# Reordering the projections around a long-convolution chain, with turns of four, later gates, a shorter root and interleaved last tiles, in a two-layer hybrid mixer and MoE kernel

## The reference

```python
h = modulate(layer_norm(x))                      # adaLN shift and scale, per stream
z = h @ w_in                                     # A: q 512, k 128, v 128; B: q, k, v 256 each; C: 3 x 256
A = dense_attention(rope(rms(q)), rope(rms(k)), v)      # 8 heads, 2 kv heads
B = neighbourhood_attention(q, k, v, rpb)               # 4 heads
x0, x1, v = split(short_conv(z_C, 3 taps))              # C: hyena
u = v * x1;  C = (long_conv(u, filters) + u * skip) * x0     # by transforms of length 512
x = layer_norm(alpha * x + gate * (concat(A, B, C) @ w_out))
```

## Time and profile before

| | us |
|---|---|
| median of 3 runs | 1529.31 (1528.60 to 1532.37) |
| the profiled execution, its own time | 1529.05 |
| its span, first to last instruction | 1527.2 |
| mean granted TensorE clock | 0.928 |
| PE busy | 1320.1 (86%) |
| VectorE, ACT, GpSimd busy | 538.8, 290.7, 303.7 |

### The profile page before, as it was taken

One profiled execution on the slowest core, in us unless ns is written; L12 is line 12 of the kernel. 1 busy time (PEld: TensorE's weight loads), 2 busy tenths in 40 slices (PEclk: granted clock), 3 DMA queues, 4 the chain that ended last, 5 costly groups with the idle time before them and its releaser, 6 DMA issues. The chain is left out here.

```text
span 1527.2 us, 19670 instructions
## 1 busy us (share of the span) xinstructions
PE 1320.1 (86%) x6420; PEld 733.0 (48%) x6421; DVE 538.8 (35%) x1346; ACT 290.7 (19%) x711; POOL 303.7 (20%) x395
## 2 busy tenths in 40 slices
PE   4999997788879999989889689994985799999991
PEld 1443433444445566656556434473543554545440
DVE  5205014456574322213222109245457221111124
ACT  0100001433210122212222211112520011111110
POOL 0000001445203133323232200100610411111000
PEclk9899997899897999999999989997996799999995
DMA  9767669000225899999998296423023799999930
GB/s 339 289 265 283 240 249 309 1 1 1 97 97 187 322 375 376 366 374 373 384 377 331 105 349 257 172 99 101 1 97 124 263 399 387 402 407 400 408 143 28
DMA packets 109724, 373.32 MB, mean 244 GB/s; under 512 B 17946, under 2 KB 24348, under 8 KB 100408
## 3 DMA queue, kind: packets, MB, share of 16 engines
q1 hardware_dynamic: 85752, 313.51, 54.5%
q0 software_dynamic: 23008, 55.40, 9.8%
q10 hardware_dynamic: 864, 3.15, 0.5%
HBM read 368.78 MB, written 30.47 MB: 261 GB/s over the span
## 5 line engine op out<-in xcount | busy, mean ns | idle before, releaser
L1239 PE MATMUL bank<-weights,b_qk 128*64 128x256 f32 (+2 forms) x1040 | 160.2, 384 | 4.4 <-DVE b_qk L2114 2.5
L1239 PEld LDWEIGHTS bank<-weights,b_qk 128*64 128x64 f32 (+2 forms) x1040 | 110.9, 147 | 63.9 <-issue 36.5
L2120 DVE TENSOR_TENSOR expert_act<-silu_a,bank 128x128 f32<-128x128 f32 x76 | 21.9, 288 | 310.7 <-ACT silu_a L1529 310.7
L1271 PE MATMUL bank<-tokens_h,a_k 128*128 128x512 f32 x208 | 103.7, 622 | 0.0
L1261 PE MATMUL bank<-weights,expert_act_T 128*64 128x512 f32 (+2 forms) x260 | 91.8, 617 | 8.6 <-DMA weights<-in_exp_w 4.9
L2308 POOL DMA_INDIRECT shift_scale_gate_norm<-scratch_h,gather_index x82 | 84.8, 1034 | 71.3 <-POOL gather_index L2305 66.6
L1239 PE MATMUL bank<-features_h,b_qk 128*32 128x256 f32 (+2 forms) x512 | 95.2, 381 | 0.4
L1059 PE MATMUL bank<-weights,features_h 128*128 128x512 f32 x192 | 86.2, 604 | 0.8 <-ACT features_h L1342 0.8
L2114 DVE COPY b_qk<-bank 128x512 f32<-128x512 f32 x78 | 53.9, 692 | 80.7 <-PE bank L1227 80.6
L1227 PE MATMUL bank<-tab,shift_scale_gate_norm 128*128 128x128 f32 x624 | 82.2, 275 | 0.0
L1529 ACT ACTIVATE silu_a<-bank 128x128 f32<-128x128 f32 x76 | 21.1, 278 | 315.0 <-PE bank L1239 315.0
(11 more groups left out here) (325 smaller groups left out, 2021.4 us busy)
## 6 DMA issues: line engine op xcount, KB each, us to landing
weights<-in_exp_w SPq DMA_DIRECT2D x195, 512.0 KB, 10.4
shift_scale_gate_norm<-in_ada_w SPq DMA_DIRECT2D x48, 1024.0 KB, 6.7
features_h<-in_exp_w SPq DMA_DIRECT2D x64, 512.0 KB, 9.7
qkv<-in_exp_w SPq DMA_DIRECT2D x64, 512.0 KB, 15.0
a_q<-in_exp_w SPq DMA_DIRECT2D x32, 512.0 KB, 12.4
weights<-in_w_in SPq DMA_DIRECT2D x6, 2048.0 KB
shift_scale_gate_norm<-scratch_mod POOLq DMA_DIRECT2D x16, 512.0 KB, 8.9
probs_T<-in_exp_w SPq DMA_DIRECT2D x16, 512.0 KB, 15.5
```

Of the source, the lines that this page charges most:

```text
L1239: mm = pe.matmul(ab[r, 0:2 * HIDDEN].rearrange("p (m h) -> p m h", m=2), XGT[:, u.slot() % 2, k, r], expert_w13(slot)[:, :, k, :], start=k ...
L1271: mm = pe.matmul(ACC[g][h][:, :], GROW[:, u.slot() % 2, g * P:(g + 1) * P], YSB[:, u.slot() % 2, h * HALF:(h + 1) * HALF], start=False, st ...
L2120: tt(ACTV[:, :], SIL[:, :], ab[:, HIDDEN:2 * HIDDEN], ALU.mult).then_inc(L["act"], 1)
```

## The change

1. **Order around the hyena chain.** Ring order of w_in becomes 0, 1, 3, 4, 2. The c products stand before the b products; the b products 0 and 1 behind the q/k transposes, 2 behind the transposes of u, 3 behind the first scores, and `yh` behind that, on all engines. The short convolution works f by f as each c product is drained. x0 and u lie in the free half of piece 4's ring slot, x1 in the `probs` tile. The slot is given back to w_out only when `yh` has been drained. The 40 adaLN steps of n = 1 to 5 are spread 2, 3, 2 to 3, 3 per product; `ADAB` lies in the router's tile, so router_w is loaded after the last group is filled.
2. **Turns of four.** `more` is rounded to whole turns, one test stands around four bodies, and layer 0's first overflow block (`ALWAYS = (1, 0)`) stands in `SEQUENCE[0]`. With these inputs no turn is run in either layer.
3. **Gates behind choices (layer 1).** The one-hots come first, 8 x 62 columns; GpSimd makes only the products with the choices; VectorE multiplies with the gates; PE does the 16 choice products, then the shared expert's second product, then the 16 gate products. GpSimd's zeroing of the gather tiles stands before its waits.
4. **Shorter root.** 8 steps instead of 11 for single tiles.
5. **Last tiles.** A signal per tile from PE, tiles 2 and 3 interleaved on VectorE, each written in two halves.

The diff, cut to its core:

```diff
+ALWAYS = (1, 0)
+BLOCKS = tuple(n + EXTRA + UNROLL for n in UNITS)
+    for n in range(ALWAYS[l]):
+        seq.append((UNITS[l] + n, [(x + n, EXPERTS + n)]))
+ADA_Q, ADA_KV, ADA_C, ADA_BQK = (2, 2, 2, 2), (3, 3, 3, 3), (2, 2, 2, 2, 3, 3), (3, 3, 0, 0)
...
-        items += [("win", l, b) for b in range(5)] + [("mixc", l), ("wo", l, 0), ("wo", l, 1)]
+        items += [("win", l, b) for b in (0, 1, 3, 4, 2)] + [("mixc", l), ("wo", l, 0), ("wo", l, 1)]
...
+                if n >= RING and items[n - RING][0] == "win" and items[n - RING][2] == 4:
+                    sp.wait_ge(by_vector, jobs.of[("yh", items[n - RING][1], 1)][2])
+                            sp.wait_ge(ada_filled, DEPTH * ADA_GROUPS)
...
-                if l == 0:
-                    for k in range(KD):
-                        ada(5, k)
-                    pe.wait_ge(ada_read, DEPTH * ADA_GROUPS)
...
+                queries_keys(0)
+                queries_keys(1)
                 pe.wait_ge(u_ready, l + 1)
+                u_rows = gate_and_u(l)
...
+                queries_keys(2)
                 read_out(("uT", l, full[-1]))
...
                 for i in range(n + PV_LAG):
                     if i < n:
                         scores(i)
+                    if i == 0:
+                        queries_keys(3)
+                        long_conv()
+                        read_out(("bqk", l, 3))
+                    if l == 0 and i == PV_LAG:
+                        pe.wait_ge(ada_read, DEPTH * ADA_GROUPS)
...
-                dve.wait_ge(by_scalar, jobs.of[("c", l, 5)][2])
+                for f, z in enumerate((*x0, *x1, *us)):
+                    dve.wait_ge(by_scalar, jobs.of[("c", l, f)][2])
...
                 with pe.Fori(0, EXTRA_TURNS) as i:
-                    for c in range(every, every + UNROLL):
-                        with pe.If(i * UNROLL + (c - every) < more):
+                    with pe.If(i * UNROLL < more):
+                        for c in range(every, every + UNROLL):
...
+                free(ts(turns, b[0:1, LISTED - EXPERTS:LISTED - EXPERTS + 1], float(UNROLL - 1 - ALWAYS[l]), float(EXTRA), ALU.add,
+                        ALU.min))
+                link(ts(turns, turns, int(math.log2(UNROLL)), None, ALU.logical_shift_right))
+                link(ts(turns, turns, int(math.log2(UNROLL)), None, ALU.logical_shift_left))
...
-                if l == DEPTH - 1:
-                    for _ in gates_of_choices():
-                        pass
+                if l == DEPTH - 1:
+                    gates = gates_of_choices()
+                    for _ in range(TOP_K):
+                        next(gates)
+                    gated(0)
+                    shared_act(nt - 1, full[-1])
...
+                if summed:
+                    for _ in gates:
+                        pass
+                    gated(1)
...
+            def rsqrt_steps(var, t):
+                xh, y, w = NV[:, t:t + 1], RS[:, t:t + 1].bitcast(F32), NT[:, t:t + 1]
+                yield ts(xh, var, -0.5, -0.5 * EPS, ALU.mult, ALU.add)
+                yield ts(RS[:, t:t + 1], xh.bitcast(I32), -0.5, float(0x1EF759DF), ALU.mult, ALU.add)
+                for _ in range(3):
+                    yield stt(w, y, xh, y, ALU.mult, ALU.mult)
+                    yield stt(y, w, 1.5, y, ALU.add, ALU.mult)
...
+                    one, two = finished(0), finished(1)
+                    for _ in range(5):
+                        next(one)
+                    for _ in one:
+                        next(two, None)
+                    for _ in two:
+                        pass
```

More of the change, by code:

```diff
@@ L281, in plan @@
             jobs.add(("kv", l, t), "scalar")
-        for f in range(4):
-            jobs.add(("bqk", l, f), "scalar")
         for f in range(6):
@@ L794, in ada, with ada_steps @@
                     mm.then_inc(ada_filled, 1)
+            ada_at = [KD]
+            def ada_steps(many):
+                for _ in range(many):
+                    ada(*divmod(ada_at[0], KD))
+                    ada_at[0] += 1
             def filter_layer(l, n):
@@ L929, in _, with queries_keys @@
                     if l == 0:
-                        ada(2, 2 * t)
-                        ada(2, 2 * t + 1)
+                        ada_steps(ADA_KV[t])
                 first = full[0] * P
-                w = arrived(("win", l, 2)).rearrange("p (k c) -> p k c", k=KD)
-                for f in range(4):
+                for f in range(6):
+                    w = arrived(("win", l, 3 + f // 4)).rearrange("p (k c) -> p k c", k=KD)
+                    b = start(("c", l, f))
+                    for k in range(KD):
+                        mm = pe.matmul(b[:, first:HALF], w[:, k, (f % 4) * P:(f % 4 + 1) * P], HT[:, k, first:HALF],
+                                       start=k == 0, stop=k == KD - 1)
+                    mm.then_inc(bank_filled, 1)
+                    if l == 0 and f == 3:
+                        columns(1)
+                    if l == 0:
+                        ada_steps(ADA_C[f])
+                def queries_keys(f):
+                    w = arrived(("win", l, 2)).rearrange("p (k c) -> p k c", k=KD)
                     lo = first if f < 2 else 0
@@ L1211, in _ @@
                     mm.then_inc(shared_added, 1)
+                    for g in range(len(full)):
+                        pe.wait_ge(onehot_g, g + 1)
+                        for j in range(TOP_K):
+                            mm = pe.matmul(O_BANK[1][:, 0:BLOCKS[l]], ONE_S[:, g, j, :], ONE_B[l][g][:, j, :],
+                                           start=g + j == 0, stop=g == len(full) - 1 and j == TOP_K - 1)
+                    mm.then_inc(onehot_used, 1)
                 L = loop[l]
@@ L2169, in _, with finished, step @@
                 if l == DEPTH - 1:
-                    dve.wait_ge(sums_ready, 1)
-                    for t in full:
-                        g = full.index(t)
-                        dve.wait_ge(modg_in, 32 * (2 * l + 2))
+                    dve.wait_ge(modg_in, 32 * (2 * l + 2))
+                    dve.wait_ge(norm_in, 32 * (2 * l + 2))
+                    def finished(g):
+                        t = full[g]
+                        mu, var, y = MV[:, t, 0:1], MV[:, t, 1:2], RS[:, t:t + 1].bitcast(F32)
+                        def step(ins):
+                            steps[0] += 1
+                            ins.then_inc(vector_step, 1)
+                            return steps[0]
+                        dve.wait_ge(sums_ready, g + 1)
```

279 lines of the change are left out of this document (146 added, 133 removed).

## The result

The changed kernel takes 1452.32 us (median of 4 runs, 1448.18 to 1454.61), and the kernel before, in runs on the same chip, 1530.84 us (4 runs). The ratio is 0.9479, 95% interval 0.9444 to 0.9514: 5.2% faster. The forecast was 1458, with 1444 to 1482 around it. Six later runs of the same kernel gave 1447.66 to 1456.97, median 1451.16; all ten together have a median of 1451.4.

A forecast was written before the change was run, and what follows sets the result against it. TensorE work plus the holes between its dense stretches, and the clock at restart, were taken as the bound. Savings 22 + 21 + 7.5 + 8 + 10 + 1.2 + 2.6 - 0.8 = 71.5 us gave 1458 us, range 1444 to 1482.

The forecast's parts named there:

- Layer 0's projections: Reordered work around layer 0's hyena chain covers TensorE's waits: 22 us saved, bounds 12 and 25.5.
- the subtraction of 3.5 us for adaLN loads in the kv stretch: Layer 0's kv products: three 1 MB loads at 3.2 us each fill 9.8 us, leaving nothing for a ring load.
- the one hole that I left at 3.3 us: Layer 0, behind the inverse transform: TensorE waits 3.3 us for drains, second maxima and scaling before the second transposes.
- The best case, 25.5: Layer 0's hyena chain: 28.8 us replace 54.3, at best 25.5 us saved.
- Layer 1's, 21 forecast: Same reordering in layer 1: 16.2 us replace 38.6, u ready about evenly; 21 us saved, bounds 14 and 22.4.
- Turns of four, 7.5 and 8: Overflow loops behind the experts: fewer tests and a written block save 7.5 us in layer 0, 8 in layer 1.
- The assumption that a test costs as much as a turn: Layer 1's closing gap: 32 tests and 8 turns at 0.33 us each; 16 remain, 5.3 us.
- The rival that the turn is what costs: Overflow loops: jumps back, or one long jump, carry the cost, so 13 us of savings vanish: 1471 us; chance 0.12.
- The slower rival: Overflow loops: the longer jump over four bodies must fetch code; at 4 us more a turn, near 1537 us; chance 0.03.
- Gates, 10 forecast: Layer 1's routing: choice products first bring the first gathered tokens earlier; 12.3 us listed, 10 taken as weights may hold back.
- The rival that weights bound it: Layer 1's expert loop: queues cannot start the weight stream earlier, swallowing the 10 us saved: 1468 us; chance 0.07.
- Root, last tiles, shifts: Shorter roots save 1.2 us in layer 1, last tiles 2.6 at the end; list shifts cost 0.8 over both layers.

The follow-up runs named there:

- e1: Changed kernel with layer 0's adaLN steps bunched, ten in one go behind the c products and none behind the b products: 1464.94 us.
- e3: Changed kernel with the transposes of u moved ahead of the first two b products: 1460.24 us.
- e11: Changed kernel itself, unchanged, measured again beside a version that skips the overflow loop: 1451.16 us.
- e6: Changed kernel with one more test around the whole loop of overflow turns, on every engine: 1446.91 us.
- e10: Changed kernel with the last tiles one after the other on VectorE and the root in 11 steps again for single tiles: 1450.26 us.
- e2: Changed kernel with the fourth b product and the inverse transform ahead of the first scores, in both layers: 1477.23 us.
- e12: Changed kernel with one more test around the whole overflow loop, run again beside the unchanged changed kernel: 1446.16 us.
- e9: Changed kernel with layer 1's one-hots at 8 x 85 columns again instead of 8 x 62: 1453.36 us.

## Why the prediction was right, and where it was off

**Layer 0's projections, 22 forecast, 26.1 measured.** The plan of the stretch was right, with clock 1.00 and no wait above 1.51 us from 180 us on. The step that failed is the subtraction of 3.5 us for adaLN loads in the kv stretch. The kv products stand at 96 to 137 us, and TensorE is busy without a gap from 60 to 250.4; no load is waited for. The pace of 3.2 us a load that I took from the earlier trace rows is not what the queue can do when it is alone: e1 shows 2.4 to 2.7. And the one hole that I left at 3.3 us is 1.51. The best case, 25.5, was not quite the best. It could have been better still: at 174.58 two adaLN steps take 3.60 us at clock 0.51, where the kernel before has 1.93, so 1.7 us were lost without any wait (the rows stand in the last section).

**Layer 1's, 21 forecast, 22.9 measured.** u was ready with the end of the second b product; the weight load of its transposes waits 0.34 us. e3 shows what the cover is worth. My best case here, 22.4, was short by the softmax wait again, which is 1.26 us and not 2.

**Turns of four, 7.5 and 8.** The block in the written order gave 2.4 of 2.5 (8.91 to 6.48 us), the way from its products to the first row product 4.2 (of which 3.9, of the 5 forecast, are behind the scatter), and the expert loop ahead of it lost 3.2. That loss is the term that the sum had at nothing: 1.4 us more of waits for weights and 1.5 more of busy time at the same number of matmuls. Its cause stays open (e11). In layer 1 8.7 against 8.0. The assumption that a test costs as much as a turn was wrong in its parts, 0.44 and 0.27 or a little more against 0.33 each, and it left out the turns that cost no gap. The two errors nearly cancel, so the 8.0 was hit in part by luck. The rival that the turn is what costs is out, since 24 tests alone are 10.6 us. The slower rival is out too: the jump over four bodies costs with its turn 0.71 us and not 5, and e6's jump over the whole loop leaves a gap of 1.58. The Trainium skill, "Advanced Engine Details and Errata", Control Flow Timing, has about 108 ns for a compare-and-branch; these runs have four times that on TensorE and twice that on GpSimd for a test around a body. The rule of the Trainium skill that spoke for the slower case ("Runtime: NRT & Kernel Launch", Instruction fetch mechanics) shows no price here: the longest jump, e6's, leaves a gap of 1.58 us with no packet in it. A fetch hidden under the last matmuls is not excluded.

**Gates, 10 forecast, 12.8 measured.** I had taken 10 between 12.3 and 4.3 for weights that might hold the loop back. They did not: the loop of layer 1 is as long as before to 0.2 us. The tokens come at 17.26 us where the list gave 17.8, and that close hit is luck: the shared output took 8.75 us and not 7.1, the choices, the gates and the way to the shared factor less than listed, and in nine other versions the tokens come at 15.0 to 15.3. The lower bound was added up wrong too: its four terms make 26.0 us, so 4.1 and not 4.3 to 5. The rival that weights bound it is out.

**Root, last tiles, shifts.** 3.4 us at the end against 2.6 forecast, and e10 gives 2.8 to 3.1 of them back. TensorE's wait for the last tile's norms in layer 1 went from 3.63 us (1152.19 to 1155.82) to 2.83 (1096.75 to 1099.58): 0.8 of the 1.2 that two shorter roots were to bring; in layer 0 the last tile's transposes follow the shared product without a wait in both kernels (437.71 and 411.79), so nothing there, as forecast. The shifts cost nothing: from TensorE's first counting product to the last position product of layer 1's list are 6.31 us in both. My 0.8 for them was in the wrong place, since they lie beside those products.

**What the sum lacked.** 3.0 us came in stretches whose order is unchanged: 1.6 in layer 0's attention and routing, where the same 928 matmuls ran at clock 0.93 and not 0.90, and 1.4 in the row sums, 0.9 of it shorter waits for rows (0.37 instead of 0.25 and 1.03) and 0.5 clock. The sum of 71.5 missed the profiled 80.9 by 9.4 us: 4.1 in layer 0's projections, 2.8 for the gates, 1.9 in layer 1's projections, 3.0 in these stretches and 1.7 of smaller parts, less 4.1 in layer 0's loop and behind it. The medians saved less, 78.5 us, since the profiled execution lies 4.1 us below its median after the change and 1.8 before.

## What to carry to other kernels

Reorder work so that a dense product stands behind every chain of another engine, and give a wait of TensorE a range of prices from its own length upwards: 3.18 us of wait cost 6.1 in e2, and 2.99 us ahead of the same product cost 3.1 in the kernel before. Spread the steps that eat a stream of loads evenly over the products, and put a test on a path only around what is long; a test around the whole of a rare loop was worth 5 us, and half the turns, with half the room for overflow, gave as much. Read a small edit at its own place in the trace, for here the same kernel's runs lie 9 us apart, and take in the stretch ahead of it, since the clock can move 2 us between the two.

## What the runs showed of the hardware that was not expected

**A wait can cost twice its length, or nothing more.** In e2 TensorE ran the forward transform at clock 1.00, stood 4.14 us and then ran the inverse transform at 0.71 for 9.9 us. Windows of e2, columns as in the earlier trace rows:

```profile
241.70:245.90 4.20, 0.06 (x2) 0.07 (x1) 3.74 (x6) 0.00 (x0) 0.00 (x0) 0.88 0.00 0
245.90:255.80 9.90, 9.90 (x32) 7.97 (x32) 1.44 (x2) 0.00 (x0) 0.00 (x0) 0.71 0.00 0
```

In e1 7.5 us of wait cost 13.5, in e2's layer 1 8.7 us more of wait 15.0. But 1.51 us in the changed kernel's layer 0 left it at 1.00, and e3's 6.84 us cost 8.7. In the kernel before, a wait of 2.99 us in layer 1 left the same inverse transform at 1.00, where e2's 3.18 us made 6.52 of it:

```profile
1054.55 3.72 PE L998 MATMUL bank<-weights,c_padded 128*128 128x256 f32 x16 [2.99 <-DVE c_padded L1846]
```

**The clock can fall while TensorE is busy.** Behind 32 small products of 4 columns (3.55 us, without a wait around them) the next two adaLN steps ran at 0.51 in the changed kernel and at 1.00 in the kernel before. The changed kernel, then the kernel before:

```profile
174.58 3.60 PE L806 MATMUL bank<-shift_scale_gate_norm,probs_T 128*32 128x512 f32 x16
```
```profile
180.44 1.93 PE L786 MATMUL bank<-shift_scale_gate_norm,probs_T 128*32 128x512 f32 x16
```

The two steps take 3.20 to 3.64 us in twelve of the thirteen profiles behind the change, and e1, which has three steps there, 5.35. Why the kernel before escapes it was not tried.

**The clock comes back at different times in versions with the same code.** Behind the 13.8 to 13.9 us in which TensorE waits for layer 0's rows, the first 10 us of the same row products ran at 0.86 in the changed kernel and at 0.72 in e3, by the windows of each:

```profile
854.40:864.40 10.00, 10.00 (x20) 4.44 (x21) 0.00 (x0) 1.39 (x4) 0.00 (x0) 0.86 1.00 383
```
```profile
855.00:865.00 10.00, 9.99 (x17) 4.40 (x18) 0.00 (x0) 0.78 (x3) 0.00 (x0) 0.72 0.90 358
```

The stretch of row sums and norms took 106.3 us in the one and 109.4 in the other. It goes with the version rather than the execution, as far as two profiles each can tell: the changed kernel has 106.3 and 106.5 (e11), the one that skips the loop 109.0 and 109.2 (e6, e12). The other executions have no trace, so where the 9 us between them arise is not shown.

**A small product costs the same at 62 and at 85 columns**, 0.115 us a piece at full clock (e9).
